# Two runs of throw-away matmuls ahead of the feed-forwards of a two-block fp32 kernel, taken out

## The reference

```python
# first block
x = x + gate_m[:, None] * rmsnorm(y, g_mix_post)
h2 = rmsnorm(x, g_ff_pre) * (1.0 + scale_f[:, None]) + shift_f[:, None]
y2 = jnp.square(jax.nn.relu(h2 @ w_ff1)) @ w_ff2
x = x + gate_f[:, None] * rmsnorm(y2, g_ff_post)
# second block
x = x + rms_norm(memory_cross_attention(h, m, w_xq[l], w_xkv[l], w_xo[l]), post_x_g[l])
h = rms_norm(x, pre_ffn_g[l])
f = jnp.square(jax.nn.relu(h @ w_ff1[l])) @ w_ff2[l]
x = x + rms_norm(f, post_ffn_g[l])
```

## Time and profile before

| what | value |
|---|---|
| median of 3 runs | 794.24 us |
| the profiled execution's own time | 793.84 us |
| its span, first to last instruction | 792.4 us |
| TensorE (PE) busy | 777.2 us, 98% of the span |
| VectorE (DVE) busy | 574.1 us, 72% |
| ScalarE (ACT) busy | 432.9 us, 55% |
| GpSimd (POOL) busy | 86.9 us, 11% |
| mean granted TensorE clock | 0.999 |
| DMA | 163.61 MB, mean 206 GB/s |

### The profile page before, as it was taken

How to read it: one execution, slowest core, us unless ns; L and a number is a source line. 1 busy time by engine, 2 the same in 40 slices (tenths; PEclk the granted TensorE clock), 3 DMA queues, 4 the chain that set the end, 5 groups by cost and what they waited for, 6 DMA issues and landing times.

```text
span 792.4 us, 11548 instructions
## 1 busy us (share of the span) xinstructions
PE 777.2 (98%) x4516; PEld 675.1 (85%) x4516; DVE 574.1 (72%) x782; ACT 432.9 (55%) x644; POOL 86.9 (11%) x141
## 2 busy tenths in 40 slices
PE   6999999999999999999999999999999999999997
PEld 5999877788788888888899998889988988888885
DVE  5986999769577676777677989857556666655664
ACT  5554567663555744454465478457645644444452
POOL 5033980000100000000020000011001100000001
PEclk9999999999999999999999999999999999999999
DMA  9999988755546585855556544546433655555551
GB/s 325 367 290 310 365 283 296 276 172 188 172 153 220 178 297 188 282 198 184 181 165 219 181 145 135 174 159 210 145 99 107 217 197 195 188 187 189 198 171 54
DMA packets 83605, 163.61 MB, mean 206 GB/s; under 512 B 5456, under 2 KB 13840, under 8 KB 83552
## 3 DMA queue, kind: packets, MB, share of 16 engines
q1 hardware_dynamic: 81632, 157.31, 58.7%
q10 hardware_dynamic: 1424, 4.81, 1.8%
q0 software_dynamic: 496, 0.76, 0.5%
HBM read 161.81 MB, written 1.05 MB: 206 GB/s over the span
## 4 chain that ended last, share of the span: by engine, by line
PE 91%; DVE 3%; issue 2%; ACT 1%; DMA 1%; SPq 1%; POOL 1%; DVEq 0%; POOLq 0%; ACTq 0%
PE bank L1831 20%; PE bank L1833 19%; PE bank L1832 19%; PE bank L1896 13%; PE bank L1899 7%; PE bank L1844 2%; PE bank L1850 2%; PE bank L1846 2%; DVE ada_acc L1023 1%; DMA raw_ring<-in_w_in 1%; PE bank L1938 1%; PE bank L2496 1%; PE bank L2090 1%; SPq L486 1%; DVE lo_ring L993 1%
## 5 line engine op out<-in xcount | busy, mean ns | idle before, releaser
L993 DVE TENSOR_TENSOR lo_ring<-raw_ring,hi_ring 128x1024 fp32r<-128x1024 f32 x248 | 305.3, 1237 | 147.1 <-ACT hi_ring L532 146.4
L532 ACT CAST hi_ring<-raw_ring 128x1024 fp32r<-128x1024 f32 x248 | 259.3, 1051 | 254.1 <-PE bank L1833 150.4
L1831 PE MATMUL bank<-hi_ring,branch_hi 128*128 128x512 f32 x352 | 139.1, 395 | 0.0
L1832 PE MATMUL bank<-lo_ring,branch_hi 128*128 128x512 f32 x352 | 137.2, 390 | 0.0
L1833 PE MATMUL bank<-hi_ring,branch_lo 128*128 128x512 f32 x352 | 137.1, 389 | 0.0
L1896 PE MATMUL bank<-h_hi_lo,hi_ring 128*128 128x512 f32 x448 | 111.8, 392 | 0.0
L1896 PEld LDWEIGHTS bank<-h_hi_lo,hi_ring 128*128 128x128 f32 x448 | 81.3, 189 | 15.0
L1833 PEld LDWEIGHTS bank<-hi_ring,branch_lo 128*128 128x128 f32 x352 | 66.1, 188 | 14.0
L1831 PEld LDWEIGHTS bank<-hi_ring,branch_hi 128*128 128x128 f32 x352 | 66.1, 188 | 13.8 <-issue 0.7
L1832 PEld LDWEIGHTS bank<-lo_ring,branch_hi 128*128 128x128 f32 x352 | 66.2, 188 | 13.4 <-issue 0.5
L1831 PE MATMUL bank<-h_hi_lo,hi_ring 128*128 128x256 f32 x240 | 69.2, 288 | 0.0
(11 more groups left out here) (293 smaller groups left out, 1182.3 us busy)
## 6 DMA issues: line engine op xcount, KB each, us to landing
raw_ring<-in_w_ff SPq DMA_DIRECT2D x128, 512.0 KB, 3.5
raw_ring<-in_w_in SPq DMA_DIRECT2D x64, 512.0 KB, 4.7
raw_ring<-in_w_out SPq DMA_DIRECT2D x16, 512.0 KB, 3.3
raw_ring<-in_w_xkv SPq DMA_DIRECT2D x16, 512.0 KB, 3.5
mem_v<-in_w_ada SPq DMA_DIRECT2D x12, 512.0 KB, 5.4
mem_k<-in_w_ada SPq DMA_DIRECT2D x12, 512.0 KB, 5.7
ada_ring<-in_w_ada SPq DMA_DIRECT2D x8, 512.0 KB, 6.2
raw_ring<-in_w_branch SPq DMA_DIRECT2D x8, 512.0 KB, 3.2
```

Source lines behind the costliest of these rows:

```text
L532: act.copy(m.hi[:, m.slot(u)], m.raw[:, m.slot(u)]).then_inc(s.hi_done, 1)
L993: dve.tensor_tensor(m.lo[:, m.slot(u)], m.raw[:, m.slot(u)], as_f32(m.hi[:, m.slot(u)]), ALU.subtract).then_inc(s.lo_done, 1)
L1831: pe.matmul(out, a_hi, b_hi, start=start, stop=False, skip_group_check=True)
L1832: pe.matmul(out, a_hi, b_lo, start=False, stop=False, skip_group_check=True)
```

## The change

`keep_busy` and the argument `idle` are removed, with both uses. TensorE issues 22 matmuls and 22 weight loads fewer, and no longer claims bank 0 at that place.

```diff
-    def keep_busy(n):
-
-        if n:
-            claim(0)
-        for _ in range(n):
-            pe.matmul(bank[0][:, :], m.h_hi[:, 0, 0:P], m.h_both[:, 0].rearrange("p a s -> p (a s)"), start=True, stop=True)
-
-    def turn_normed(turn, idle=0):
+    def turn_normed(turn):
         claim(4, 5, 6, 7)
         for tt in range(NT):
-            if tt:
-                keep_busy(idle)
             n = KD // turn.halves[tt]
...
-    def turn_x(turn, post, idle=0):
+    def turn_x(turn, post):
         claim(4, 5, 6, 7)
         for tt in range(NT):
-            if tt:
-                keep_busy(idle)
             for n in range(2):
...
-    turn_normed(s.ff1t, idle=16)
+    turn_normed(s.ff1t)
...
-    turn_x(s.ff2t, s.post_x, idle=6)
+    turn_x(s.ff2t, s.post_x)
```

## The result

The changed kernel takes 796.45 us (median of 8 runs, 795.77 to 797.05) where the kernel before takes 794.33 us beside it: 1.0027 times as long, with a 95% interval of 1.0016 to 1.0037. That is 2.1 us more for 22 matmuls fewer. Four single executions in this document, three of them of the kernel before, took 1294 to 2740 us, and are left out of the ratios, means and counts.

A forecast was written before the change was run, and what follows sets the result against it. The prediction took TensorE to bound the kernel from FF1's first matmul on. To the runs' median of 794.24 us it added 2.2 at FF1 and 0 at FF2, giving 796.4 us, range 794.0 to 798.8 us.

The forecast's parts named there:

- The 22 matmuls at 0, since they were on no chain: Ahead of FF1 and FF2: removing 3.91 + 1.62 us of TensorE work beside other engines' work is worth 0 at unchanged clock.
- Everything lost at FF1 arrives at the end: From FF1's first matmul on, every microsecond TensorE loses in a dense stretch arrives at the end; no wait swallows it.
- The clock falls ahead of FF1: Ahead of FF1, TensorE stands 3.93 us and its clock falls from 2.4 to 1.2 GHz; at FF1 alone, chance 0.50.
- Its price, 2.2 us: The fall at FF1 costs 0.25 us at tile 1's transposes and 1.95 us in the lead matmuls, together 2.2 us.
- The first transposes: At FF1, tile 1's first two transposes, which release the first VectorE step, come 0.25 us later if the clock falls.
- The lead unit: At FF1, the lead matmuls run at half rate for 3.9 us and lose half of that, 1.95 us.
- The signs that were named in advance: Right: clock 0.50 beginning between 217.8 and 223.4 us, ending 2 to 4 us behind FF1's lead start; 1.00 around FF2.
- FF2 at 0: Ahead of FF2, 1.91 us of standing costs 0, being well below the 3.9 us seen to bring the fall.
- The Trainium skill's rule on transposes: Transposes do not count as TensorE being busy as matmuls do; by it FF2 falls too, 4.4 us instead of 2.2.
- the rival of two falls: The clock falls at both FF1 and FF2, costing 4.4 us: 798.6 us; chance 0.25.
- The rival that the clock holds at both places: At FF1 and FF2 TensorE keeps 2.4 GHz and nothing changes: 794.2 us; chance 0.22.
- That the kernel gets faster: The throw-away matmuls held something up; without them less than 0.27 us is gained, about 794.0 us; chance 0.03.

The follow-up runs named there:

- ff1_kept: The kernel before without the 6 matmuls ahead of FF2, the 16 ahead of FF1 kept: 794.41 us median, ratio 1.0008.
- run with twelve: The kernel before with 12 instead of 16 matmuls ahead of FF1, the 6 ahead of FF2 kept: 794.49 us, ratio 1.0006.
- ff2_kept: The kernel before without the 16 matmuls ahead of FF1, the 6 ahead of FF2 kept: 795.73 us, ratio 1.0020.
- run with eight: The kernel before with 8 instead of 16 matmuls ahead of FF1, in one group, the 6 ahead of FF2 kept: 795.53 us, ratio 1.0015.

## Why the prediction was right, and where it was not

The forecast of 796.4 us meets 796.45, and in the two profiled executions of the changed kernel (796.43 and 796.44 us) its two terms are about as they were said: 2.15 and 1.90 us at FF1, 0 at FF2. That the median is met to 0.05 us is luck all the same. In the runs that take the places one at a time FF1 costs 1.54 us in the mean and FF2 0.66 us: the one term was too large, the other, put at 0, too small.

*The 22 matmuls at 0, since they were on no chain.* Right. The wait ahead of tile 1 ends with L1043 before and after, tile 1's transposes lag by the same 0.34 us as all that stands ahead of them, and in the executions that did not fall (six of ff1_kept, eight of the run with twelve) the time is that of before.

*Everything lost at FF1 arrives at the end.* Right: the lag of 2.49 us at FF2's transposes is still 788.92 - 786.43 = 2.49 us at the last matmul:

```profile
788.92 0.39 PE L1833 MATMUL bank<-hi_ring,branch_lo 128*128 128x512 f32 x1
```

*The clock falls ahead of FF1.* Right, in every execution of ff2_kept. *Its price, 2.2 us*, was over-sized in the mean: 1.54 us in ff2_kept, with single executions from 1.0 to 2.3. The trace of the changed kernel that is shown above has 2.15, and its parts stand beside the prediction's. The first transposes: 0.25 us were said, and the lead unit starts 223.99 - 222.06 = 1.93 us behind tile 1's transposes where it was 1.68, so 0.25. That this is met is luck, since the way to it is not the one that was given; the chain that ended last goes through all eight transposes into the lead unit, not through VectorE's L1057 behind the first two:

```profile
221.52 0.50 DVE gates L1043
222.06 1.97 PE bank L1938 x8
224.03 0.51 PE bank L1844
```

The lead unit: 3.9 us at the low level were said, at half rate; it ran 228.20 - 223.99 = 4.21 us at 0.21 us of spacing where 0.12 is usual, so it lost 1 - 0.12/0.21 = 0.43 of that time and not 0.50, which is 1.8 us. A longer low stretch and a smaller loss in it nearly make up for each other; 0.1 us of the 2.15 is in neither part.

How much of the low stretch falls on the lead unit differs between the three traces without matmuls ahead of FF1. The stretch is 6.8 us long in each, but it begins at different moments, and the lead unit ran at the low level for 3.6, 4.2 and 4.4 us; FF1 cost 1.90, 2.15 and 2.25 us (the second execution of the changed kernel, the first, and that of ff2_kept).

*The signs that were named in advance.* Most came as said: the fall in the window that was named, the doubled spacing, the wait for L1043, the clock of 1.00 around FF2 (in these two executions). One sign of being wrong came too, "a low stretch of more than 6 us": it lasts 6.8 us and ends 4.2 us behind the lead unit's start, where 2 to 4 were said. The length of 3.9 us, taken from the kernel's first matmuls, did not carry over: here TensorE was at work again from 222.06 on, 6.1 us before the clock rose. The sum came out near all the same because it counted the lead matmuls alone. (Its upper end, 3.3 us, is 3.2 by its own terms: half of 5.85, and 0.25.)

*FF2 at 0.* This is the step that failed, although neither profiled execution of the changed kernel shows it, and with it the reason that was given for it: that 1.91 us of standing is well below the 3.9 us seen to bring the fall. The fall at the end of the kernel showed a stand that is enough, and I read it as one that is needed. It was one value out of a wide spread, too. In the changed kernel's own trace the last matmul ends at 788.92 + 0.39 = 789.31, and the clock falls at about 791.4, after 2.1 us:

```profile
789.40:791.00 1.60, 0.00 (x0) 0.00 (x0) 0.75 (x1) 0.69 (x2) 0.65 (x2) 1.00 0.00 0
791.10:794.90 3.80, 0.00 (x0) 0.00 (x0) 1.42 (x2) 0.00 (x0) 0.14 (x1) 0.54 0.37 138
```

Over the 14 traces of this case that last stand lasts from 2.0 us (the run with twelve) to 5.3 us (the run that takes FF2's transposes out of the way) before the clock falls. The run with eight falls after 2.08 us ten times in 11, and FF2 after 1.89 us six times in 15, at 0.66 us in the mean of the first 11.

*The Trainium skill's rule on transposes*, the ground on which the rival of two falls rested. The rival came out half true (FF2 does fall, sometimes), but not for that reason: 32 transposes in place of the 16 matmuls hold the clock in all 11 executions. The Trainium skill, "TensorE: Matmul & The Clock Gate", Part 4: PE-mode transpose, says that they do not count in the same way; for these float32 transposes the measurement decides against it. Whether transposes of other types hold the clock no run here shows.

*The rival that the clock holds at both places* is out for FF1 where nothing fills the stand, and holds for FF2 in 9 of 15 executions. *That the kernel gets faster* is out: with the clock kept, no run was faster than before by more than its interval. None of the runs gave a version that beats the kernel before.

## What to carry to other kernels

Where TensorE bounds the stages behind it, a stretch that is mostly standing costs more than its own length: first the wait, then dense work at half the clock (1.8 to 4.4 us of it in the six traces with a fall), and that second part is bought off by work that nobody reads, as long as that work ends before the data that TensorE waits for arrive. Count float32 transposes as such work, and do not take a stand of 2 us for safe because a longer one was seen to precede a fall elsewhere. Work that is spread over the stand held the clock oftener here than as much work in one group (seven executions of 11 against one). And time it over many executions: whether a half-filled stretch loses its clock differs from one execution of the same program to the next, so that a median can show 0.15 us of loss where the mean is 0.66 us.

## What the runs showed of the hardware that was not expected

The fall does not come at a fixed distance from the beginning of a stand: in the changed kernel's trace it comes at 221.4, still in the stand, 3.3 us after its beginning; in the slower profiled execution of ff1_kept it comes at 610.3, 2.9 us after the stand's beginning, when TensorE has been back at work for almost a microsecond (its transposes start at 609.34).

At the end of the kernel, where nothing follows, it comes 2.0 to 5.3 us after the last matmul. The low stretch is 6.8 us long in the three traces without matmuls ahead of FF1, and 3.4 us in the three others with a fall (eight in one group, and the two at FF2).

The same eight matmuls keep the clock in one of 11 executions in one group, and in seven of 11 in two groups; three executions in 11 fall with twelve, none of 79 of the kernel before, with its sixteen (the highest of the 79 is 794.66 us).
